# Eight ring slots and nine places for the context's PEER rows, arguments and masks moved from VectorE to ScalarE and GpSimd, and two projections of the first head moved into the context's stage

## The reference, cut to what matters

```
h  = rms_norm(x) * (1 + scale1) + shift1
bg, cg, xg, q, k, v, og, i, f = split(h @ w_in)
conv  = bg * conv3(cg * xg)                        # short convolution, 4 x 128 columns
mlstm = 4 heads, forward and backward, chunkwise:  # head width 128
  dmat = where(tril, b_t - b_s + i_s, -inf);  m = max(b_t + m_prev, max(dmat))
  s    = (q @ k.T) * exp(dmat - m)
  num  = a * (q @ C) + s @ v ;  den = a * (q @ n) + sum(s)
  h    = num / max(|den|, exp(-m));  C, n are carried from chunk to chunk
x  = x + gate1 * (concat(conv, mlstm * sigmoid(og)) @ w_out)
h2 = rms_norm(x) * (1 + scale2) + shift2
PEER: 8 heads x 16 picks of 16384 experts for each token
  a = <h2, u[e]> ;  w = softmax(gate) * gelu(a) ;  y = sum of w * v[e] over 128 picks
x  = x + gate2 * y ;  final rms_norm
```

## Time and profile before

| | us |
|---|---|
| median of 3 runs | 3599.26 (3594.08 to 3601.49) |
| profiled execution, its time | 3597.29 |
| profiled execution, its span | 3595.5 |
| mixer stage in the span | 307.1 to 860.1 |
| peer stage's prologue | 860.1 to 949.3 |
| peer stage's loop | 949.3 to 3595.5 |
| mean granted clock of PE | 0.935 |

### The profile page before, as it was taken

One profiled execution on the slowest core, in us unless ns is written; L12 is line 12 of the kernel. 1 busy time (PEld: TensorE's weight loads), 2 busy tenths in 40 slices (PEclk: granted clock), 3 DMA queues, 4 the chain that ended last, 5 costly groups with the idle time before them and its releaser, 6 DMA issues.

```text
span 3595.5 us, 33409 instructions
## 1 busy us (share of the span) xinstructions
PE 2992.0 (83%) x10068; PEld 1519.9 (42%) x10068; DVE 2539.2 (71%) x6056; ACT 911.7 (25%) x2291; POOL 1532.8 (43%) x1301
## 2 busy tenths in 40 slices
PE   5985988895488888898888898888988888988887
PEld 4753444442244434443443444344434434443343
DVE  3457775884766777777777767777777776677765
ACT  1211111011122322322232223223322322232222
POOL 0003554442444444444444444444444444444443
PEclk8987989897799999999999999999999999999999
DMA  8554776676999999999999999999999999999998
GB/s 347 179 162 176 255 267 237 244 287 229 367 419 412 408 420 419 412 401 416 407 411 420 419 412 406 420 413 407 403 412 420 415 419 412 412 401 420 419 412 340
DMA packets 227809, 1317.53 MB, mean 366 GB/s; under 512 B 24688, under 2 KB 44592, under 8 KB 95024
## 3 DMA queue, kind: packets, MB, share of 16 engines
q0 software_dynamic: 184320, 1208.04, 83.0%
q1 hardware_dynamic: 43312, 107.36, 8.2%
HBM read 1305.29 MB, written 10.01 MB: 366 GB/s over the span
## 4 chain that ended last, share of the span: by engine, by line
DVE 31%; PE 20%; DMA 17%; issue 3%; ACT 3%; DVEq 2%; POOL 0%; POOLq 0%
PE acc L1504 15%; DMA room<-in_uv,expert 15%; DVE room L1742 14%; PE mix L1470 3%; PE ps_q L1448 2%; DVE wt L1655 2%; ACT gelu L1561 2%; DMA room<-in_uv,room 2%; DVE work L1639 1%; DVE work L1635 1%; DVE picked L1642 1%; DVE ind L1603 1%; DVE ind L1596 1%; DVE work L1597 1%; DVE pos L1623 1%
## 5 line engine op out<-in xcount | busy, mean ns | idle before, releaser
L1504 PE MATMUL acc<-room,diag 128*128 128x512 f32 x4096 | 1939.1, 622 | 391.5 <-ACT diag L1567 391.4
L1434 POOL DMA_INDIRECT room<-in_uv,expert x1024 | 1243.5, 1214 | 1382.1 <-PE acc L1504 1194.6
L1742 DVE CUSTOM_DVE_ANT_0 room<-room,h 128x1024 f32<-128x1024 f32 x1024 | 1229.7, 1221 | 356.2 <-DMA room<-in_uv,expert 354.2
L1504 PEld LDWEIGHTS acc<-room,diag 128*128 128x128 f32 x4096 | 781.0, 198 | 1450.9 <-issue 1450.1
L1567 ACT ACTIVATE diag<-ident,wt 128x128 f32<-128x128 f32 x1024 | 377.4, 397 | 508.3 <-PE acc L1504 399.0
L1561 ACT ACTIVATE gelu<-dot 128x2 f32<-128x2 f32 x512 | 104.4, 204 | 1196.5 <-DVE dot L1742 1195.2
L1008 PE MATMUL region<-hT_then_w_out,w 128*128 128x512 f32 x800 | 368.0, 621 | 44.2 <-DVE seen L1195 43.6
L996 POOL DMA_INDIRECT room<-in_uv,cexpert x223 | 252.7, 1133 | 243.1 <-DVE acc L1181 121.8
L1655 DVE SCALAR_TENSOR_TENSOR wt<-gelu,rz,ex 128x2 f32<-128x2 f32 x512 | 113.4, 221 | 273.9 <-ACT gelu L1561 273.9
L1008 PEld LDWEIGHTS region<-hT_then_w_out,w 128*128 128x128 f32 x800 | 158.5, 201 | 245.5 <-issue 245.5
L1448 PEld LDWEIGHTS ps_q<-h2T,wq 128*128 128x128 f32 x2048 | 240.2, 193 | 31.2 <-issue 31.2
(11 more groups left out here) (301 smaller groups left out, 2005.9 us busy)
## 6 DMA issues: line engine op xcount, KB each, us to landing
w<-in_w_in SPq DMA_DIRECT2D x49, 512.0 KB, 4.7
room<-in_w_ada SPq DMA_DIRECT2D x12, 2048.0 KB, 17.5
room<-in_uv,expert POOLq DMA_INDIRECT x1024, 11.3
room<-in_wq SPq DMA_DIRECT2D x8, 1024.0 KB, 7.2
wq<-in_wq SPq DMA_DIRECT2D x1, 7168.0 KB, 45.9
xt<-in_x SPq DMA_DIRECT2D x9, 512.0 KB, 19.3
out_y<-x SPq DMA_DIRECT2D x9, 512.0 KB, 8.2
room<-in_w_out SPq DMA_DIRECT2D x2, 2048.0 KB, 11.5
```

The source lines that it names most:

```text
L1434: nc.gpsimd.indirect_dma_start(out=uv[:, k % RING, :], out_offset=None, in_=t["uv"], in_offset=bass.IndirectOffsetOnAxis(ap=expert[:, h % ...
L1504: last = nc.tensor.matmul(acc[i % 2][:, a * BANK:(a + 1) * BANK], diag[:, k % DIAG, :], uv[:, k % RING, D + a * BANK:D + (a + 1) * BANK], ...
L1742: last = nc.vector.tensor_tensor_reduce(out=uv[:, k % RING, 0:D], in0=uv[:, k % RING, 0:D], in1=h2[:], scale=1.0, scalar=0.0, op0=ALU.mult ...
```

## The change

1. The ring for the context's rows has 8 slots in place of 6 (rows 13 and 14 of `room` are added).
2. `BESIDE` has nine places for each head in place of six. 245 rows (128 dots, 117 of the `v` rows) stand in the mixer in place of 223; 11 are left for the peer stage's prologue in place of 33, and all of them stand behind the choice (`BESIDE_MIX`, `BESIDE_QUERY` are 0).
3. `arguments(d)` goes from DVE to ACT: eight Relu with scale -1 and the column as bias, then Exp with scale -1. `kw` goes to ACT too, as eight copies with a scale. To that end the columns are negated when the context's stage copies them.
4. The mask goes from DVE to POOL: two affine_selects of 128 x 1024 for each head, one into a new tile `sT_back` (backward), one in place in `sT` (forward). They stand in POOL's queue after 12 of the head's gathers (`MASK_AFTER`), and wait until ACT has evicted "s".
5. `weights(1)` stands behind the convolution and four rows; four rows stand between the product cg x xg and `combine(0)`.
6. GELU is applied in head 1 behind its Sqrt, not in head 2 ahead of its Exp.
7. Head 0's projections og and cg are made at the end of the context's stage, behind the last scores, with ACT's Sigmoid and copy ahead of the last `soften`.

```diff
-    BESIDE = ((17, 10, 7, 6, 9, 15), (17, 10, 7, 6, 9, 15), (16, 9, 7, 6, 9, 14), (17, 10, 7))
-    GELU_HEAD = 2
+    BESIDE = ((22, 5, 7, 4, 4, 3, 7, 4, 13), (22, 5, 7, 4, 4, 3, 7, 7, 10), (22, 5, 7, 4, 4, 3, 7, 4, 13),
+              (22, 5, 7, 4))
+    MASK_AFTER = 12
+    GELU_HEAD = 1
...
                 for k in range(PICKS + V_PICKS):
+                    if k - MASK_AFTER in starts:
+                        wait_evicted(pool, starts.index(k - MASK_AFTER), "s")
+                        nc.gpsimd.affine_select(out=sT_back[:], in_=sT, compare_op=ALU.is_ge, fill=0.0, base=0,
+                                                pattern=[[0, NL], [-1, P]], channel_multiplier=1)
+                        pool.drain()
+                        nc.gpsimd.affine_select(out=sT, in_=sT, compare_op=ALU.is_ge, fill=0.0, base=0,
+                                                pattern=[[0, NL], [1, P]], channel_multiplier=-1).then_inc(masked, 1)
                     if k >= RS:
                         pool.wait_ge(c_read, k - RS + 1)
...
                     def exps(d):
-                        wait_evicted(act, h, f"u{d}")
-                        nc.scalar.activation(seen[:], seen[:], ACT.Exp).then_inc(exped, 1)
+                        act.wait_ge(jobs_done, job_done(h, f"u{d}"))
+                        for c in range(NL):
+                            last = nc.scalar.activation(seen[:, c, :], tiles(f"u{d}")[:, c], ACT.Relu, scale=-1.0,
+                                                        bias=cols[:, d, 0, c + 1, h:h + 1])
+                        last.then_inc(free[region_of(f"u{d}")], 1)
+                        act.drain()
+                        nc.scalar.activation(seen[:], seen[:], ACT.Exp, scale=-1.0)
+                        act.drain()
+                        end = P - 1 if d == 0 else 0
+                        for c in range(NL):
+                            last = nc.scalar.activation(kw[:, c, :], ktok[:, c, :], ACT.Copy,
+                                                        scale=seen[:, c, end:end + 1])
+                        last.then_inc(weighted, 1)
                         evict(f"a{d}", qa, tiles(f"a{d}"))
...
                     def weights(d):
-                        dve.wait_ge(exped, h * 2 + (d + 1))
-                        wait_evicted(dve, h, "ktok")
+                        if d == 0:
+                            dve.wait_ge(masked, h + 1)
+                        dve.wait_ge(weighted, h * 2 + (d + 1))
                         wait_evicted(dve, h, f"a{d}")
                         nc.vector.tensor_copy(dec[:], qa[:, :, end])
-                        nc.vector.tensor_tensor(kw, ktok, seen[:, :, end:end + 1].to_broadcast([P, NL, P]),
-                                                ALU.mult).then_inc(weighted, 1)
...
+                project_first(3, OG)
+                project_first(4, CG)
...
-    BESIDE_MIX, BESIDE_QUERY = 16, 7
+    BESIDE_MIX, BESIDE_QUERY = 0, 0
```

More of the change, by code:

```diff
@@ L624, in _ @@
                         soften(h - 1)
+                act.wait_ge(q_done, 5)
+                act.wait_ge(first_done, 4)
+                nc.scalar.activation(og0, pp[1][:], ACT.Sigmoid).then_inc(first_taken, 1)
+                act.wait_ge(first_done, 5)
+                nc.scalar.copy(cg0, pp[0][:]).then_inc(first_taken, 1)
                 soften(PH - 1)
@@ L844, in region_of, with jobs_until, evicted @@
     return BODY.index(name) % 2
[L847 to L851, removed]
+ELSEWHERE = {(0, "og"), (0, "cg")} | {(HEADS - 1, name) for name in HANDED_ON}
+JOBS = [(h, name) for h in range(HEADS) for name in BODY if (h, name) not in ELSEWHERE]
+def jobs_until(h, name):
+    at = (h, BODY.index(name))
+    return [(g, x) for g, x in JOBS if (g, BODY.index(x)) <= at]
 def job_done(h, name):
-    return h * NJ + (BODY.index(name) + 1 - left_out(h, name))
+    return len(jobs_until(h, name))
+def evicted(h, name):
+    r = region_of(name)
+    return r, 1 + sum(region_of(x) == r for _, x in jobs_until(h, name))
 def region_free(h, name):
[L862 to L870, removed]
+    r, value = evicted(h, name)
+    return r, value - ((h, name) in JOBS)
 def mixer_stage(nc, ctx, t, ident, hT, s, cx, wo, gfin, wo_in):
@@ L991, in _ @@
                     nc.gpsimd.memset(t["junk"][:, 2 + d:3 + d], 1.0).then_inc(mixed_out[d], 16)
+                starts = [sum(map(sum, BESIDE[:h])) for h in range(HEADS)]
                 for k in range(PICKS + V_PICKS):
+                    if k - MASK_AFTER in starts:
[5 more added lines that the diff above has]
+                                                pattern=[[0, NL], [1, P]], channel_multiplier=-1).then_inc(masked, 1)
                     if k >= RS:
@@ L1190, in body @@
                 def body(h):
[L1191 to L1197, removed]
                     def weights(d):
                         end = P - 1 if d == 0 else 0
[L1202 to L1203 removed]
+                        if d == 0:
+                            dve.wait_ge(masked, h + 1)
+                        dve.wait_ge(weighted, h * 2 + (d + 1))
                         wait_evicted(dve, h, f"a{d}")
                         nc.vector.tensor_copy(dec[:], qa[:, :, end])
[L1206 to L1207 removed]
                         dve.drain()
                         nc.vector.tensor_tensor(qa, qa, by_tile(qT[:]), ALU.mult)
[L1210 to L1213 removed]
+                        nc.vector.tensor_tensor(seen[:], seen[:], sT_back[:] if d else sT, ALU.mult).then_inc(ready, 1)
                     def chain(d):
@@ L1251, in body @@
                         .then_inc(free[region_of("xg")], 1)
+                    beside(h, 3)
                     combine(0)
-                    arguments(1)
-                    weights(1)
                     nc.vector.tensor_scalar(y[:], u, conv[:, h, 1:2], conv[:, h, 3:4], ALU.mult, ALU.add)
@@ L1265, in body @@
                         dve.drain()
-                    beside(h, 3)
+                    beside(h, 4)
+                    weights(1)
+                    beside(h, 5)
                     chain(1)
-                    beside(h, 4)
+                    beside(h, 6)
                     dve.wait_ge(jobs_done, job_done(h, "bg"))
```

52 lines of the change are left out of this document (28 added, 24 removed).

## The result

The changed kernel takes 3601.65 us (3598.62 to 3608.21, 20 runs) against 3597.21 (3589.95 to 3602.53, 20 runs): a ratio of 1.0013, 95% interval 1.0007 to 1.0019. This is within 0.2% of no change and a little slower, where 3580 was forecast. The profiled execution has a span of 3598.1 us in place of 3595.5.

What follows compares the result with a forecast made beforehand. In heads, DVE's rows and PE's k waiting for `combine(0)` were taken to bind; the loop, DMA busy, stayed unchanged. Terms +5.9 - 7 + 6 - 9 + 12 - 25 = -17 from 3597.3 gave 3580 us, range 3558 to 3594.

Steps and rivals of the forecast that it cites:

- 1.26 at 1024, 2.5 for the pair: POOL's two mask selects in heads 1 to 3: 1.26 us each, scaled from 0.63 at 512 elements; upper end 5.3 for both.
- Rival A: POOL's selects are dear, delaying row 13 in heads 1 to 3: time same or longer; chance 0.15, 0.08 slower than 3606.
- signs that I had named for being wrong: Selects over 2 us each, k no later than +72, a prologue over 75 us, a loop that isn't 2646 us.
- Head 1: Mixer's head 1: k starts about +81 in place of +71.5, with a shorter tail; length about 146.5, +6 us (-2 to +10).
- Head 0: Mixer's head 0: 13.4 us of DVE go, five rows (6.4 to 7.5) come; -7 us (-14 to -3).
- og and cg no longer stand in PE's way: Part of the head 0 term: two projections moved to the context's end free PE there; no size of its own.
- +4.4 at the context's end: Two projections of 13.9 us on an idle PE, then copy, table load and softmax: forecast +5.9 us (+4 to +8).
- Heads 2 and 3: Mixer: head 2 -9 us (-15 to -6), GELU's 23.15 us wait gone; head 3 +12 (+6 to +15), the stall and four rows.
- the wait for "s" and the stall behind it: POOL waits for ACT's eviction of "s", so DVE stalls 14 to 15 us for row 13, three times, in heads 1 to 3.
- the work taken from DVE: Arguments, masks, weighted keys and DVE's waits for ACT leave DVE: 13.4 us a head for two directions.
- the prologue (-25.3 for -25): Peer stage's prologue: residual starts 26.3 us earlier without 16 context rows ahead, one more row behind costs 1.4; -25 us (-27 to -18).
- Rivals B and C: B: DMA traffic keeps the prologue long, time the same, 0.08. C: stall mostly absorbed, k as early as before, 3545 to 3566, 0.17.

## Why the prediction was wrong

The step that failed is a size: "1.26 at 1024, 2.5 for the pair". The selects were right: 1.09 each, and a line through two sizes in the trace of before (0.29 at 128, 0.63 at 512) gives 1.08. But the drain between them stood in the diff and I gave it no price. Like the selects it lies ahead of every later gather. It makes the pair 8.0 to 8.1 us in heads 1 to 3 and 10.3 in head 0, 5.5 to 7.8 us more than the 2.5. Taken away it gives back 22.7 us, where the miss is 21.7 (3601.65 less 3580). That the two agree so closely is in part luck, since head 0 also misses for another reason.

Rival A came nearest: it said that the gain is gone when the pair takes 8.2 us. But it made the selects dear, and they were not. I gave it 0.15, since I read the trace's 0.63 us of one select as the price of the step. The drains in the trace of before have no gather ahead of them, so no row there could give 5.8 us; what was owed was a term for the drain with an open upper end. None of the signs that I had named for being wrong showed: the selects take under 2 us, k comes at +80, the prologue is 63.9 us and the loop 2645.1.

Head 1 fits (+7.1 for +6), but for two reasons that cancel, which is luck. "s" was evicted 19.0 us into the head in place of 21.8 and the landing was quicker (4.3 us from the gather's start to its dot, where I took 6 to 7), which gave back most of the drain's 5.8.

Head 0 misses by 8, and the drain explains only 4 of it (144.4 us without it against 148.1, from first transpose to first transpose). There the masks did not come before DVE needed row 13: it waited 5.37 us for that row. The other 4 us are open. The step "og and cg no longer stand in PE's way" is not where they went, for it had no size of its own (13.4 us of DVE less 6.4 to 7.5 of rows is the -7 already). Nor did og and cg stand in PE's way: PE waited 25.48 us for DVE there, and without a drain the head is within 0.7 us as long with them as without. So +4.4 at the context's end was paid for next to nothing. The term also has no entry for the place of the four rows ahead of `combine(0)`. Their move takes 5.2 us out of head 0 (148.1 to 142.9), which would cover the rest; no run separates it.

Heads 2 and 3 miss by 6.6 and 6.9. Without the drain they are 7.5 and 6.9 us shorter, so nothing is left to explain there.

Right were: the wait for "s" and the stall behind it, the wait of k for `combine(0)` and a tail of 65 to 70 us, GELU's stall gone, the work taken from DVE (49.4 us by experiment for the part that was put at 44, PE's waits included), and the prologue (-25.3 for -25). Rivals B and C had nothing in their favour: the prologue is 63.9 us, and PE's busy time was never the bound.

## What to carry to other kernels

Work put into another engine's queue is paid by all that stands behind it there, so look first at what that engine waits for at that place: ten gathers later the same masks cost 40 us less. Price every line that the change adds to a queue, the drains too; one that the trace of before doesn't show gets an upper bound that is not zero. And if a row of work is put ahead of a short step for which another engine waits, it is the whole head that gets later.

## What had not been expected of the hardware

A drain on POOL that follows indirect gathers took 5.77 us where the last gather had been issued 8 to 16 us before (heads 1 to 3 of the change), and 6.7 to 8.4 us where it lay 1 to 3 us back (head 0, and all heads with the masks after 22). It is paid once: a second drain cost 0.1 to 0.6 us, and a drain ahead of the wait hid it. In head 0 of the run with the first projections back the same drain took 1.13 us. It ended 9.4 us after the last gather's end there, against 8.8 in head 0 of the change and 9.4 in head 0 of the run with a drain ahead of the wait. But in head 1 of the change it ended 14.3 us after the last gather, so what sets the price is not settled.

Selects and dots hold each other up. POOL and then DVE in head 1 of the run with masks after 22 and no drain:

```profile
477.63 1.41 POOL L1012 TENSOR_SCALAR_AFFINE_SELECT sT_back<-room 128x1024 f32<-128x1024 f32 x1
479.00 2.07 POOL L1014 TENSOR_SCALAR_AFFINE_SELECT room<-room 128x1024 f32<-128x1024 f32 x1
```

```profile
478.14 1.98 DVE L1216 CUSTOM_DVE_ANT_0 room<-room,ch 128x1024 f32<-128x1024 f32 x1
480.05 2.10 DVE L1216 CUSTOM_DVE_ANT_0 room<-room,ch 128x1024 f32<-128x1024 f32 x1
```

The pair takes 3.4 us in place of 2.2, and the two dots that begin beside it take 1.98 and 2.10 in place of 1.22. The page "SBUF — State Buffer" of the Trainium skill (section "SBUF: two separate sides") says that whichever of the two sides starts first shuts the other out for the whole instruction. For selects and dots this trace agrees: the dots lose 1.6 us to this pair, where the prediction had estimated 2.5 in head 0. In the changed kernel itself no dot begins beside a select, and all 128 lie between 1.21 and 1.29 us. Gathers make no dot longer there, though they get longer themselves beside dots.
